# Load order at the launch of a two-layer hybrid backbone: `c` first on its own semaphore, two modulation halves ahead of four constants, `x` behind the first half

## What is computed

```python
mod_l = (jax.nn.silu(c) @ w_ada[l] + b_ada[l]).reshape(b_, 1, N_MOD, D_MODEL)
mod_c = (jax.nn.silu(c_ctx) @ w_ada[l] + b_ada[l]).reshape(N_MOD, D_MODEL)
...
def _pre(x, nw, shift, scale):
    return rmsnorm(x, nw) * (1 + scale) + shift

def swiglu(h, w_in_ff, w_out_ff):
    gu = h @ w_in_ff
    g, u = gu[..., :D_FF], gu[..., D_FF:]
    return (jax.nn.silu(g) * u) @ w_out_ff
```

## Time and profile before

| | us |
|---|---|
| median of 3 runs | 2886.11 |
| lowest and highest | 2883.41, 2886.54 |
| the profiled execution, its own time | 2884.53 |
| its span, first to last instruction | 2882.7 |
| TensorE busy | 2712.7 (94%) |
| VectorE busy | 1462.9 (51%) |
| ScalarE busy | 864.7 (30%) |
| GpSimd busy | 114.6 (4%) |
| mean granted TensorE clock | 0.975 of full |

### The profile page before, as it was taken

The page is one execution under the profiler, slowest core; times in us unless marked ns, Lnnn a source line. Parts: engine busy times, 40 slices in busy tenths (PEclk is TensorE's granted clock), DMA queues, the critical chain, the costliest instruction groups (busy, mean ns, idle before and its releaser), DMA issues.

```text
span 2882.7 us, 35922 instructions
## 1 busy us (share of the span) xinstructions
PE 2712.7 (94%) x14392; PEld 2438.0 (85%) x14392; DVE 1462.9 (51%) x1967; ACT 864.7 (30%) x1144; POOL 114.6 (4%) x92
## 2 busy tenths in 40 slices
PE   5999998998987989999999999999998988699998
PEld 1999997887966789999988899999887766688887
DVE  2555555654545665555466655554454655532333
ACT  3211112343432441111235511113353523422232
POOL 0000000001200110000001100000011100100001
PEclk9999999999989999999999999999999989899999
DMA  5333334432200233333343333333332201322232
GB/s 209 131 116 116 119 123 155 144 132 81 71 19 1 88 112 134 118 116 131 110 168 132 117 117 121 133 127 114 122 126 93 92 1 47 129 90 100 102 117 73
DMA packets 100975, 313.19 MB, mean 109 GB/s; under 512 B 6929, under 2 KB 23313, under 8 KB 87313
## 3 DMA queue, kind: packets, MB, share of 16 engines
q1 hardware_dynamic: 93744, 297.20, 29.9%
q10 hardware_dynamic: 7136, 14.68, 1.5%
HBM read 309.76 MB, written 2.10 MB: 108 GB/s over the span
## 4 chain that ended last, share of the span: by engine, by line
PE 86%; DVE 8%; issue 2%; ACT 2%; DMA 1%; POOL 0%; SPq 0%; POOLq 0%; DVEq 0%; ACTq 0%
PE ps L1563 46%; PE ps L1577 24%; PE ps L793 5%; PE ps L1606 2%; DVE w_lo L1300 2%; PE ps L899 1%; PE ps L1635 1%; PE ps L1645 1%; PE ps L883 1%; PE ps L874 1%; ACT w_hi L1093 1%; DVE arena L565 1%; DVE acc L1326 1%; PE ps L1619 1%; PE ps L892 1%
## 5 line engine op out<-in xcount | busy, mean ns | idle before, releaser
L1563 PE MATMUL ps<-xn_hi,w_hi 128*128 128x384 f32 (+2 forms) x2528 | 724.9, 342 | 21.0 <-DVE arena L1385 9.5
L1563 PE MATMUL ps<-xn_lo,w_hi 128*128 128x384 f32 (+2 forms) x2528 | 721.1, 340 | 0.0
L1563 PE MATMUL ps<-xn_hi,w_lo 128*128 128x384 f32 (+2 forms) x2528 | 721.0, 340 | 0.0
L1300 DVE TENSOR_TENSOR w_lo<-raw,w_hi 128x2048 fp32r<-128x2048 f32 x211 | 499.8, 2369 | 396.0 <-ACT w_hi L1093 395.8
L1563 PEld LDWEIGHTS ps<-xn_hi,w_hi 128*128 128x128 f32 x2528 | 463.9, 189 | 33.0 <-issue 16.5
L1093 ACT ACTIVATE w_hi<-raw 128x2048 fp32r<-128x2048 f32 x211 | 400.5, 1898 | 302.4 <-PE ps L1577 225.6
L1563 PEld LDWEIGHTS ps<-xn_lo,w_hi 128*128 128x128 f32 x2528 | 465.1, 189 | 11.2
L1563 PEld LDWEIGHTS ps<-xn_hi,w_lo 128*128 128x128 f32 x2528 | 464.9, 189 | 11.3
L1196 ACT ACTIVATE arena<-ps 128x384 f32 (+3 forms) x158 | 72.8, 496 | 1078.0 <-PE ps L1563 1078.0
L1326 DVE SCALAR_TENSOR_TENSOR acc<-raw_ada,silu_c,acc 128x512 f32<-128x512 f32 x512 | 345.5, 745 | 4.5 <-DVE acc L1314 3.2
L1577 PE MATMUL ps<-w_hi,hj_hi 128*128 128x512 f32 x952 | 299.8, 396 | 18.8 <-DVE w_lo L1300 8.5
(11 more groups left out here) (194 smaller groups left out, 2271.9 us busy)
## 6 DMA issues: line engine op xcount, KB each, us to landing
raw<-w_ff_in SPq DMA_DIRECT2D x104, 1024.0 KB, 5.2
raw<-w_ff_out SPq DMA_DIRECT2D x77, 1024.0 KB, 4.9
raw_ada<-w_ada SPq DMA_DIRECT2D x128, 512.0 KB, 3.8
raw<-w_out SPq DMA_DIRECT2D x16, 1024.0 KB, 4.8
raw<-w_in SPq DMA_DIRECT2D x12, 1024.0 KB, 5.3
arena<-w_ada SPq DMA_DIRECT2D x4, 2048.0 KB, 17.6
gate_row<-norm_w ACTq DMA_DIRECT2D x12, 512.0 KB, 4.3
x<-x_in ACTq DMA_DIRECT2D x6, 512.0 KB, 6.9
```

Source lines behind the costliest of these rows:

```text
L1300: nc.vector.tensor_tensor(w_lo[par][:, 0:width], raw[par][:, 0:width], w_hi[par][:, 0:width].bitcast(F32), ALU.subtract).then_inc(S["w_lo" ...
L1563: ins = mm(ps[:, 4 * b + part + c, col:col + wd], w[:, k, c, :], xx[:, k, t0:t0 + wd], start=(k == 0 and i == 0), stop=(k == KC - 1 and i ...
```

## The change

SP now sends `cvec` alone on a new semaphore `c_in`, then three constants, halves 0 and 1, the other four constants, half 2, the weight slot, half 3. ScalarE computes `silu_c` as soon as `c_in` is there, and issues the six loads of `x` only when half 0 has landed. VectorE still waits for all the other seven constants before the mask, and makes the six reciprocals behind the first two row copies. The low part of weight slot 0 goes ahead of the fourth row copy instead of between the third copy and its bias.

```diff
-            "consts pool_consts dve_consts x_in "
+            "c_in consts pool_consts dve_consts x_in "
@@ SyncE
-            for dst, src in ((cvec[:], cvec_in), (b_col[:], b_col_in), (nw_col[:], nw_col_in), (convw[:], convw_in),
-                             (convb[:], convb_in), (hn_w[:], hn_w_in), (tri, tri_in), (gate_b[:], gate_b_in)):
-                sp.dma_start(dst, src).then_inc(S["consts"], 16)
-            for i in range(4):
-                if i == 3:
-                    load(0, 0, w_ff_in[0, 0, 0])
+            def first_half(i):
+
                 src = w_ada[0].rearrange("(k p) n -> p k n", p=P)[:, :, i * HB:(i + 1) * HB]
                 sp.dma_start(ada0(i), src).then_inc(S["ada_first"][i], 16)
+
+            sp.dma_start(cvec[:], cvec_in).then_inc(S["c_in"], 16)
+            for dst, src in ((b_col[:], b_col_in), (nw_col[:], nw_col_in), (tri, tri_in)):
+                sp.dma_start(dst, src).then_inc(S["consts"], 16)
+            first_half(0)
+            first_half(1)
+            for dst, src in ((convw[:], convw_in), (convb[:], convb_in), (hn_w[:], hn_w_in), (gate_b[:], gate_b_in)):
+                sp.dma_start(dst, src).then_inc(S["consts"], 16)
+            first_half(2)
+            load(0, 0, w_ff_in[0, 0, 0])
+            first_half(3)
@@ ScalarE
+            act.wait_ge(S["c_in"], 16)
+            nc.scalar.activation(silu_c[:], cvec[:], ACT.Silu).then_inc(S["silu_c"], 1)
+            act.wait_ge(S["ada_first"][0], 16)
             for t in range(NT):
                 act.dma_start(x[:, t, :], x_in[t]).then_inc(S["x_in"], 16)
-            act.wait_ge(S["consts"], 16 * 8)
-            nc.scalar.activation(silu_c[:], cvec[:], ACT.Silu).then_inc(S["silu_c"], 1)
@@ VectorE
-            dve.wait_ge(S["consts"], 16 * 8)
+            dve.wait_ge(S["consts"], 16 * 7)
             dve.wait_ge(S["pool_consts"], 2)
             nc.vector.tensor_copy(ident_bf[:], ident[:])
             nc.vector.tensor_scalar(mask[:], tri, -1.0, -NEG, ALU.add, ALU.mult).then_inc(S["dve_consts"], 1)
-            for t in range(NT):
-                prenorm_rs(t, t)
             for i in range(4):
-
+                if i == 2:
+                    for t in range(NT):
+                        prenorm_rs(t, t)
+                if i == 3:
+                    split_w(0, 0)
                 dve.wait_ge(S["rows_mm"], i + 1)
                 nc.vector.tensor_copy(acc[0:2, i % 2, :], ps[0:2, 5, :]).then_inc(S["rows_sb"], 1)
-                if i == 2:
-                    split_w(0, 0)
                 finish_col(i, i, 6)
```

## The result

| | before | changed |
|---|---|---|
| median of 20 runs, us | 2885.08 | 2890.84 |
| lowest and highest, us | 2881.29, 2894.37 | 2888.28, 2894.56 |
| span of the profiled execution, us | 2882.7 | 2889.5 |
| mean granted TensorE clock | 0.975 | 0.974 |

The ratio of the changed kernel to the one before is 1.002, with a 95% interval of 1.0013 to 1.0027: 5.8 us slower by the medians, 6.8 by the two spans. Single executions of one kernel differ by several us, so the launch is read from the traces and the time from the medians.

A forecast was written before the change was run, and what follows sets the result against it. The prediction took TensorE, busy 94%, to be bound at launch by its first multiplication's inputs; queue steps moved its start from 18.20 to 25.2, so 7.0 us on the 2886.1 median gave 2893.1, range 2885 to 2897.

The forecast's parts named there:

- The mechanism: Launch: TensorE's first multiplication waits for the mask, hence `gate_b` behind half 1; 75%, 5 to 9 us slower.
- Steps 1 and 2: SP's queue: half 0's issue ends at 2.6 us, against 4.67, and it lands at 10.5, against 18.07.
- Step 3: ScalarE issues `x` at 10.5; it flows from 11.8, with 1.14 MB of halves 0 and 1 left.
- Step 4: Half 1 and `x` alternate packets, 560 pairs in 8.9 us; half 1 is through at 20.7.
- Step 5: Four constants behind half 1: 2.2 us beside the rest of `x`, 0.3 us alone, through at 23.2.
- Steps 6 and 7: `gate_b` lands at 24.6; wait and mask take 0.5 us, and TensorE starts at 25.2, against 18.20.
- The lag: Time from last bytes moved to landing, taken as 1.4 to 1.5 us for `gate_b`.
- What I costed at nothing: Other moved work: mean squares, reciprocals, scalings, slot 0's parts, halves 2 and 3, clock; all expected to add no time.
- the cover: 4.3 us between slot 0's low part ending at 54.6 and the fourth copy due at 58.9; any excess adds.
- The clock: TensorE's lower level after the wait between transposes, 0.53 granted at 60 to 65 us before, should recur.
- `gate_b` does not queue behind the halves: Rival: small constants pass half 0's bytes, TensorE starts at 10.6, 6.6 us faster, 2879.5; chance 7%.
- `x` hardly hinders half 1: Rival: sharing favours SP's queue, 1.2 us faster, or goes by bytes, 1.8 us slower; together 14%.

The follow-up runs named there:

- experiment 1: Changed kernel, four late constants on their own semaphore, awaited behind the fourth row copy; mask waits for three constants: 2877.8 us against 2883.8 before, ratio 0.9976.
- experiment 3: Changed kernel with the six loads of `x` issued at once, not behind half 0: 2890.5 us against 2883.8 before, ratio 1.0024.
- Experiment 5: Kernel before with only VectorE's part: reciprocals behind two row copies, slot 0's low part ahead of the fourth: 2884.9 us against 2885.2 before, ratio 0.9999.
- experiment 2: Changed kernel with all seven other constants ahead of half 0, waits as they are: 2882.3 us against 2883.8 before, ratio 0.9994.
- experiment 4: Changed kernel with `x` issued only when half 1 has landed: 2887.8 us against 2883.8 before, ratio 1.001.
- experiment 6: Changed kernel, but SyncE issues half 2 and what follows only when half 1 has landed: 2890.1 us against 2885.2 before, ratio 1.0018.
- experiment 7: Changed kernel, half 0 right behind `cvec`, late constants on their own semaphore, TensorE awaiting the mask behind four halves: 2881.0 us against 2885.2 before, ratio 0.9983.
- experiment 8: Changed kernel, mask waiting for three constants alone and `x` issued at once: 2885.5 us against 2885.2 before, ratio 1.0001.

## Why the prediction was right, point by point

The forecast was 7.0 us slower, 2893.1, range 2885 to 2897; the median came out at 2890.84, 5.8 us slower. Of the 2.3 us between the two times, 1.0 is the median of before, which was 2886.11 over three executions and is 2885.08 over twenty.

- *The mechanism.* The mask, and TensorE behind it, waits for `gate_b`, which now stands behind half 1. Shown by the chain of the changed kernel and, causally, by experiment 1: take the four late constants out of the wait, and TensorE starts at 10.63.
- *Steps 1 and 2, half 0.* Issued at 2.61 as predicted. ScalarE's issue of `x` at 11.07 puts the landing at about 11.0; I had 10.5.
- *Step 3, `x` starts.* **Mis-sized.** I took 1.3 us from issue to first packet, from a moment when the queues were empty; behind running halves it is 3.7 us (14.81 behind 11.07).
- *Step 4, half 1 against `x`.* Follows from it: I had half 1 meet `x` for 8.9 us and get through at 20.7. It ran alone until 14.8, when 89 of its 1024 packets were left; its issue began at 3.08 and it landed 15.2 us later, at 18.3.
- *Step 5, the small constants.* **Mis-sized the other way.** With half 1 nearly through, all four met `x`: 401 packets against 406 in 18 to 22 us. I had 2.2 us beside `x` and 0.3 alone; 5.5 us lie between the landings of half 1 and `gate_b`. The 152 ns for each small packet, which I set aside as the upper bound, is about what they paid: 32 on each engine make 4.9 us, an estimate. The errors of steps 3 to 5 cancel: `gate_b`'s last packet moved at 23.06, and I had 23.2. That is not chance alone, since nearly the same bytes stand ahead of `gate_b` either way (691 of the 768 packets of `x` had moved by then), and experiment 3 comes out alike with `x` in yet another place. But the course that the prediction told, half 1 slowed by `x` and the constants quick behind it, is not what happened. SyncE's issue of the first late constant also took 3.68 us (3.71 to 7.39), for which the sum had nothing; it cost nothing, since `gate_b` was issued at 8.48, long before its turn.
- *Steps 6 and 7.* The lag was **mis-sized**: `gate_b` landed 0.7 us behind its last packet, at 23.77, and not 1.4 to 1.5 behind it, at 24.6. This is nearly all by which the start was forecast too late. Mask and start followed in 0.55 us, about as in the sum. The start is 24.32 against 25.2 predicted: 6.1 us late, not 7.0, and with the 0.3 us of the first half 6.4 at the transposes.
- *What I costed at nothing.* The reciprocals ran at 43.34 (I had about 44), the scalings ended at 49.9, slot 0's low part at 54.0 and the fourth copy was due at 58.35: the cover held, by 4.35 us. Experiment 5 shows the move itself to cost nothing that can be measured. Experiments 2 and 4 show what the cover is worth: when TensorE starts early and `x` late, this chain is the bound.
- *The clock.* After the wait between transposes TensorE ran below full clock again, 0.71 granted in 65 to 70 us and 0.50 in 70 to 75, as it had 0.53 in 60 to 65 before: shifted with the rest, at the same cost within 0.2 us (the first 48 feed-forward matmuls took 10.10 us against 9.96).
- *The rivals.* "`gate_b` does not queue behind the halves" was wrong in every run in which it was issued behind half 1, the changed kernel and experiments 1, 3, 4, 6, 7 and 8: it landed behind it in each. On the order of a queue the Trainium skill's page "DMA: Bandwidth & Descriptors", section "Queues, rings and completion order", has both sentences, ring order on each engine and no order of completion for each issuer; the traces go by the first. Its price was nearly right, as experiment 1 shows by another way: 6.6 us was the figure, 6.0 by the medians and 7.2 by the transposes. "`x` hardly hinders half 1" was right about half 1 by another way than it gave: the queues shared one for one (401 and 406), but `x` began when half 1 was nearly through, and it hindered the constants behind it.
- *The bandwidth.* The queues moved 298 GB/s in 2 to 10 us, a stretch that begins with small constants, and 388 to 398 GB/s from 10 to 18 us. That is above the 358 GB/s and below the 435 GB/s of the Trainium skill's page "DMA: Bandwidth & Descriptors", section "Specifications". The rate of the trace before was the right one to use.

## What to carry to other kernels

A wait on a semaphore that counts several loads lasts until the last of them has landed, and in all ten traces that was the last in queue order: when loads are moved, list for each wait what it counts and where the last one now stands. Here the load that the consumer needs, `tri`, had landed at 4.6 us, and the wait cost 13.7 us because it also counted constants of the mixer. Bytes ahead of a load on its own queue, and packets beside it on another, both delay it, and here each packet of a small transfer beside large ones paid a large one's time (5.5 us for four constants beside `x`, 0.7 without it); moving `x` back paid only in the versions in which nothing small and urgent stood behind the halves, and only as long as `x`'s own chain still fitted beside TensorE's.

## What the runs showed that I had not expected

- A transfer issued on the second queue while the first is busy with 2 KB packets has its first packet about 3.7 us after the issue: 11.07 to 14.81 in the changed kernel, 10.60 to 14.35 in experiment 6, 16.27 to 20.00 in experiment 4, 12.49 to 16.21 in experiment 2. These starts are from the packet records. With empty queues it is 1.1 us (0.75 to 1.83 in the kernel before). An issue in progress on SyncE is not the reason (experiment 6); what is stays open.
- TensorE's first half, 16 matmuls after nothing, took from 8.31 us (experiment 4) to 9.97 us (experiment 8), against about 7 us for each later half. In every kernel the first of them start about 0.85 us apart and the rest 0.43 us; it is three at the slow pace in experiment 4 and seven in experiment 8. The granted clock on the page reads 1.00 in that stretch (14 to 22 us before) and does not show it. This alone moves the launch by up to 1.7 us between kernels, and what sets the number is not shown.
